# Eighteen dots of the first token tile handed to GpSimd and ScalarE, earlier row fetches, and sixteen mid tokens in a hybrid decoder block

## What is computed

```
h = rmsnorm(x, g_ffn)
q = (h @ w_q) -> 8 heads x 2 halves of 128
v1, i1 = top_k(q0 . k1, 16);  v2, i2 = top_k(q1 . k2, 16)
sc, pos = top_k(v1[:, None] + v2[None, :], 16)     # 16 experts per head, 128 per token
gate = softmax(sc)
x += sum over the 128 experts e of  gate_e * gelu(h . u[e]) * v[e]
```

## Time and profile before

| | us |
|---|---|
| median of 3 runs | 1643.03 (1640.15 to 1643.32) |
| time of the profiled execution | 1643.77 |
| its span, first to last instruction | 1642.0 |
| PE busy | 1600.6 (97%) |
| DVE busy | 1056.9 (64%) |
| ACT busy | 430.1 (26%) |
| POOL busy | 672.0 (41%) |
| moved by DMA | 479.82 MB, mean 292 GB/s |

### The profile page before, as it was taken

One profiled execution on the slowest core, in us unless ns is written; L12 is line 12 of the kernel. 1 busy time (PEld: TensorE's weight loads), 2 busy tenths in 40 slices (PEclk: granted clock), 3 DMA queues, 4 the chain that ended last, 5 costly groups with the idle time before them and its releaser, 6 DMA issues.

```text
span 1642.0 us, 18540 instructions
## 1 busy us (share of the span) xinstructions
PE 1600.6 (97%) x6364; PEld 1053.6 (64%) x6364; DVE 1056.9 (64%) x2437; ACT 430.1 (26%) x1271; POOL 672.0 (41%) x715
## 2 busy tenths in 40 slices
PE   8999999999999989999999999999999999999998
PEld 6446444446786778989989999984444444444443
DVE  2012444431279899998988999996655566667555
ACT  2003444350110211111167877760000000000013
POOL 0002445440001474466745555555434335447530
PEclk9999999999999999999999999999999999999999
DMA  5424111105545899999999999999999999999962
GB/s 173 144 85 146 40 39 39 40 27 166 157 148 167 338 378 375 409 400 387 392 394 409 409 407 409 406 403 392 409 409 409 409 409 410 409 409 398 409 227 103
DMA packets 133274, 479.82 MB, mean 292 GB/s; under 512 B 14859, under 2 KB 15883, under 8 KB 133180
## 3 DMA queue, kind: packets, MB, share of 16 engines
q0 software_dynamic: 74880, 272.66, 42.2%
q1 hardware_dynamic: 58300, 205.97, 33.6%
HBM read 475.38 MB, written 3.19 MB: 291 GB/s over the span
## 4 chain that ended last, share of the span: by engine, by line
PE 72%; DVE 15%; issue 4%; DMA 4%; POOL 3%; ACT 1%; DVEq 0%; SPq 0%; POOLq 0%; ACTq 0%
PE psum L1948 27%; PE psum L1929 9%; DVE arena L1355 7%; PE psum L1739 6%; PE psum L1615 4%; DMA arena<-in_u,eidx 4%; PE psum L1763 3%; PE psum L1815 3%; PE psum L1775 3%; PE psum L1916 3%; PE psum L1858 2%; PE psum L1699 2%; PE psum L1714 2%; POOL arena L609 1%; PE psum L1685 1%
## 5 line engine op out<-in xcount | busy, mean ns | idle before, releaser
L1929 PE MATMUL psum<-arena 128*128 128x248 f32 x2048 | 444.6, 375 | 10.4 <-ACT arena L782 6.8
L1948 PE MATMUL psum<-arena 128*128 128x512 f32 x1024 | 441.8, 594 | 2.7 <-DVE arena L1413 2.7
L1929 PEld LDWEIGHTS psum<-arena 128*128 128x128 f32 x2048 | 386.1, 191 | 50.0 <-issue 12.6
L609 POOL DMA_INDIRECT arena<-in_u,eidx x256 | 256.2, 1001 | 371.9 <-DVE arena L1110 168.0
L609 POOL DMA_INDIRECT arena<-in_v,eidx x256 | 260.7, 1018 | 287.0 <-DVE arena L1390 172.0
L1948 PEld LDWEIGHTS psum<-arena 128*128 128x128 f32 x1024 | 194.9, 191 | 248.3 <-issue 246.0
L1355 DVE CUSTOM_DVE_ANT_0 arena<-psum,arena 128x1024 f32<-128x1024 f32 x256 | 303.5, 1221 | 30.9 <-DMA arena<-in_u,eidx 18.9
L1390 DVE SCALAR_TENSOR_TENSOR arena<-arena,wts 128x1024 f32<-128x1024 f32 x175 | 222.9, 1286 | 109.5 <-DMA arena<-in_v,eidx 101.7
L598 POOL TENSOR_SCALAR arena<-arena 128x256 f32<-128x256 f32 (+4 forms) x128 | 105.9, 846 | 250.9 <-DVE arena L1064 191.7
L1739 PE MATMUL psum<-arena 128*128 128x512 f32 x256 | 118.4, 605 | 0.0
L1815 PE MATMUL psum<-arena 128*128 128x256 f32 x512 | 113.0, 379 | 0.2
(11 more groups left out here) (222 smaller groups left out, 1449.9 us busy)
## 6 DMA issues: line engine op xcount, KB each, us to landing
arena<-in_ut SPq DMA_DIRECT2D x128, 512.0 KB
arena<-in_vd SPq DMA_DIRECT2D x128, 512.0 KB
arena<-in_wpack SPq DMA_DIRECT2D x105, 512.0 KB
arena<-in_u,eidx POOLq DMA_INDIRECT x256
arena<-in_v,eidx POOLq DMA_INDIRECT x256
arena<-in_w_pg SPq DMA_DIRECT2D x8, 512.0 KB
arena<-in_x SPq DMA_DIRECT2D x4, 512.0 KB, 4.9
arena<-bias_rows SPq DMA_DIRECT2D x8, 256.0 KB, 5.5
```

Source lines behind the costliest of these rows:

```text
L609: G.indirect_dma_start(out=row_slot(n), out_offset=None, in_=table, in_offset=bass.IndirectOffsetOnAxis(ap=picks, axis=0)).then_inc(row_ga ...
L1929: last = T.matmul(chunk_scores(c), u[:, k * P:(k + 1) * P], h2T1[:, k, 0:DN], start=(k == 0), stop=(k == KC - 1))
L1948: last = T.matmul(ps[VALUE_BANK[t] + h], mixed[:, c, t * P:(t + 1) * P], stream[:, c % SRING, h * HALF:(h + 1) * HALF], start=(c == 0), st ...
```

## The change

Eighteen dots of tile 0 (`SHARED_DOTS`) are no longer VectorE's. GpSimd multiplies the row with the tokens in place (`row_times`), and ScalarE sums the product by a Copy with an accumulator (`sum_row`). Twelve of them are the first twelve rows; ScalarE sums rows 0 to 6 after `heads_evac(0)`, rows 7 to 9 before `heads_evac(1)`, the others inside it. The slots are taken in a new order, so that the first rows go to slots that are free before the merge is done, and each first fetch waits only for the merges that its slot needs (`gates_gone`). The merges are moved ahead of a part of the top-k work on VectorE. `MID` goes from 8 to 16, so the dense scores have 240 columns and 8 more rows of `u` are gathered, 528 rows in all where there were 520. `EARLY_DOTS` is 144, and the steps of the top-k work lie 5 rows apart from row 12 on. `hn[0]` and `hn[1]` change places, since GpSimd needs `hn[0]` longer. PE's values wait for each late chunk when they come to it, and no longer for all. The dense results are added at k = 111 and 112, and the tail's pieces around them move along. Two `gate_exp` on ScalarE move from chunks 28 and 46 to 31 and 47.

```diff
-EARLY_DOTS = 142
+EARLY_DOTS = 144
+SHARED_DOTS = (0, 1, 2, 3, 4, 5, 6, 7, 8, 9, 10, 11, 18, 23, 28, 33, 38, 43)
+FIRST_DOTS = 12
+SUMMED_AT = ((10, 11), (18,), (23,), (28,), (), (33,), (38,), (43,))
+EARLY_ORDER = (0, 1, 5, 6, 7, 2, 3, 4)
+MIX_ORDER = (0, 1, 5, 2, 3, 4)
-MID = 8
+MID = 16
-DOT_OF_STEP = [2 + 6 * s if s < SPARSE_STEPS else 2 + SPARSE_STEPS + 5 * s for s in range(TOP_UNITS)]
+DOT_OF_STEP = [FIRST_DOTS + 5 * s for s in range(TOP_UNITS)]
...
+        gates_gone = (KC + 2, KC + 4, KC + 6, 2 * KC, 2 * KC, 0, 0, 0)
...
             def fetch(n, table, picks):
                 last_user = row_last_in_slot(n)
-                if last_user is not None:
-                    pool.wait_ge(row_used, last_user + 1)
+                if last_user is None and gates_gone[slot_of(n)]:
+                    pool.wait_ge(merged, gates_gone[slot_of(n)])
+                if last_user in SHARED_DOTS:
+                    pool.wait_ge(row_summed, SHARED_DOTS.index(last_user) + 1)
+                elif last_user is not None:
+                    pool.wait_ge(row_used, vector_rows(last_user) + 1)
...
                 if n == 0:
-                    pool.wait_ge(merged, 2 * KC)
                     pool.wait_ge(experts_known, 1)
...
+            def row_times(n):
+
+                if n == 0:
+                    pool.wait_ge(rows_normed, TILES + 1)
+                pool.wait_ge(row_gathered[slot_of(n)], 16 * times_filled(n))
+                G.tensor_tensor(row_slot(n), row_slot(n), hn[0], ALU.mult).then_inc(row_times_token, 1)
+
             for n in range(2 * NG * COLS + MID):
                 gather(n)
+                if n == 4:
+                    row_times(0)
+                    row_times(1)
+                if 2 <= n - 3 < FIRST_DOTS:
+                    row_times(n - 3)
+                if n - 5 >= FIRST_DOTS and n - 5 in SHARED_DOTS:
+                    row_times(n - 5)
...
+            def sum_row(n):
+                act.wait_ge(row_times_token, SHARED_DOTS.index(n) + 1)
+                col = PICK_ORDER[n]
+                A.activation(row_slot(n), row_slot(n), ACT.Copy, accum_out=dots[:, 0, col:col + 1]).then_inc(row_summed, 1)
...
                     if p:
                         score_evac(h, p - 1)
+                    if h:
+                        for n in SUMMED_AT[p]:
+                            sum_row(n)
...
             heads_evac(0)
+            for n in range(7):
+                sum_row(n)
             peer_norm(2, 4)
...
             turned_evac(h2T1, 1)
+            for n in range(7, 10):
+                sum_row(n)
             heads_evac(1)
...
-            pair_up(0, 4, 8)
             merge(1, UP_FIRST)
             merge(1, UP_FIRST + 1)
+            pair_up(0, 4, 8)
+            merge(1, UP_FIRST + 2)
+            merge(1, UP_FIRST + 3)
             top_pairs(0, 4, 8)
             number_low(0, 1)
             publish(0, 4, 8, 0, 8)
-            merge(1, UP_FIRST + 2)
-            merge(1, UP_FIRST + 3)
...
             for k in range(EARLY_DOTS):
-                dot(*divmod(k, COLS))
+                if k not in SHARED_DOTS:
+                    dot(*divmod(k, COLS))
...
-                if k == 104:
+                if k == 111:
                     add_dense(2)
-                if k == 105:
+                if k == 112:
                     add_dense(3)
...
-            pe.wait_ge(dense_gelu, CHUNKS)
+            pe.wait_ge(dense_gelu, CHUNKS - 1)
             pe.wait_ge(mix_applied, MID_FIRST)
             pe.wait_ge(mix_copied, WG)
-            pe.wait_ge(late_applied, CHUNKS - 1 - FIRST_MIX)

             def values(c, t):
+                if t == 0 and c > FIRST_MIX:
+                    pe.wait_ge(late_applied, c - FIRST_MIX)
                 for h in range(2):
+                    if c == 0 and t == 0 and h == 1:
+                        pe.wait_ge(dense_gelu, CHUNKS)
```

More of the change, by code:

```diff
@@ L187, in build, with vector_rows @@
         low_slots += -(low_slots - EARLY_DOTS) % MIX_SLOTS
-        first_mix_slot = EARLY_DOTS % SLOTS % MIX_SLOTS
+        assert EARLY_DOTS % SLOTS == 0
         def slot_of(n):
             if n < EARLY_DOTS:
-                return n % SLOTS
+                return EARLY_ORDER[n % SLOTS]
             if n < low_slots:
-                return (first_mix_slot + n - EARLY_DOTS) % MIX_SLOTS
-            lap, place_in_lap = divmod(n - low_slots, SLOTS)
-            return place_in_lap if place_in_lap >= MIX_SLOTS else (first_mix_slot + place_in_lap) % MIX_SLOTS
+                return MIX_ORDER[(n - EARLY_DOTS) % MIX_SLOTS]
+            place_in_lap = (n - low_slots) % SLOTS
+            return place_in_lap if place_in_lap >= MIX_SLOTS else MIX_ORDER[place_in_lap]
+        gates_gone = (KC + 2, KC + 4, KC + 6, 2 * KC, 2 * KC, 0, 0, 0)
+        def vector_rows(n):
+            return n - sum(1 for d in SHARED_DOTS if d < n)
         def u_row(i):
@@ L253, in build @@
         hn = [None] * TILES
-        for t in (2, 3, 0):
+        for t in (2, 3, 1):
             hn[t], ra = place(ra, [D])
-        scr = hn[0]
+        scr = hn[1]
         vals, idxu = [None] * 2, [None] * 2
@@ L267, in build @@
         assert ra <= EARLY_HOME and EARLY_HOME + 2 * D <= 120 * DT - 1808
-        hn[1], _ = place(120 * DT, [D])
+        hn[0], _ = place(120 * DT, [D])
         h2T1, h2e = place(H2, [KC, HT])
@@ L398, in build @@
         row_used = sem("row_used")
+        row_times_token = sem("row_times_token")
+        row_summed = sem("row_summed")
         rows_stashed = sem("rows_stashed")
@@ L498, in chain @@
             return 2 * c - 4, 2 * c - 2, 8, NCAND
-        match_rooms = (hn[0], hn[2], hn[3])
+        match_rooms = (hn[1], hn[2], hn[3])
         def matches(t, c):
@@ L669, in _ @@
                     after_low, after_high = [DOT_OF_STEP[step + x] + SLOTS for x in (2, 3)]
-                    if n == (SLOTS - 1 if t == 1 else DOT_OF_STEP[step - 1] + SLOTS):
+                    if n == (FIRST_DOTS + 4 if t == 1 else DOT_OF_STEP[step - 1] + SLOTS):
                         number_pairs(t)
@@ L853, in gelu_dots @@
             def gelu_dots(t):
-                act.wait_ge(row_used, u_row(COLS * (t + 1) - 1) + 1)
+                act.wait_ge(row_used, vector_rows(u_row(COLS * (t + 1) - 1) + 1))
+                act.wait_ge(row_summed, len(SHARED_DOTS))
                 A.activation(dots[:, t, :], dots[:, t, :], ACT.Gelu_apprx_tanh).then_inc(gelu_ready, 1)
@@ L931, in _ @@
                 if c == MID_GELU:
-                    act.wait_ge(row_used, MID_AT + MID)
+                    act.wait_ge(row_used, vector_rows(MID_AT + MID))
                     A.activation(mid_dots, mid_dots, ACT.Gelu_apprx_tanh).then_inc(mid_gelu, 1)
-                if c == 28:
+                if c == 31:
                     gate_exp(2)
-                if c == 46:
+                if c == 47:
                     gate_exp(3)
@@ L1371, in sum_early @@
                 dve.wait_ge(row_gathered[slot_of(n)], 16 * times_filled(n))
-                dve.wait_ge(row_used, n)
+                dve.wait_ge(row_used, vector_rows(n))
                 if k == 0:
@@ L1467, in _ @@
                     gates(1)
-                if k == EARLY_DOTS - 16:
+                if k == 130:
                     gates(2)
@@ L1546, in _ @@
                     tail_out(0)
-                if k == 104:
+                if k == 111:
                     add_dense(2)
-                if k == 105:
+                if k == 112:
                     add_dense(3)
                     tail_scale(1)
-                if k == 107:
+                if k == 114:
                     tail_turned(1)
                     tail_scale(2)
-                if k == 108:
+                if k == 115:
                     tail_turned(2)
-                if k == 120:
+                if k == 124:
                     tail_add(1)
-                if k == 122:
+                if k == 126:
                     tail_out(1)
@@ L1898, in mid_rows @@
             def mid_rows():
-                pe.wait_ge(row_used, COLS)
+                pe.wait_ge(row_used, vector_rows(COLS))
                 for k in range(KC):
```

5 lines of the change are left out of this document (2 added, 3 removed).

## The result

The changed kernel takes 1655.67 us (median of 4, 1654.84 to 1657.66) where the kernel before took 1643.17 beside it (1640.15 to 1645.41): ratio 1.0073, 95% interval 1.0058 to 1.0089. It is 12.5 us slower; 15.1 us less were forecast. Its span is 1655.9 against 1642.0.

What follows compares the result with a forecast made beforehand. PE and the DMA engines were both taken to run at their limit for 1000 us. Gains of 10 + 0.5 + 4.6 + 0 = 15.1 us off a median of 1643.0 gave 1628, range 1623 to 1634.

Steps and rivals of the forecast that it cites:

- Two waits on ScalarE: ScalarE's sums before and inside the second half's copies: dense chunks near 614 and 622, 3 us PE can just spare.
- rival C: In heads_evac(1), ScalarE waits for GpSimd's products; dense chunks start 20 us late, giving 1648; chance 0.11.
- Earlier fetches: Row fetches from 500 instead of 526.98: 6 to 7 rows ahead near 549, 8.3 us of DMA time.
- Less work on VectorE: Before the mixing: eighteen dots, 20.6 us, off VectorE; 4.4 us of unused DMA time won back.
- The port: SBUF interfaces shared by GpSimd and VectorE: no run showed how they hold each other up; nothing booked.
- The moved gate_exp cost nothing: ScalarE's gate exponentials, moved in the program: hidden under the chunks, cost nothing.
- MID = 16: Dense chunks and mixing: 6.9 us less PE on chunks 0 to 61, first mix at 829, 0.5 us booked in mixing.
- Rival A: PE is all that counts, the DMA keeping up by filled slots in the mixing: 21.6 us gained, 1621; chance 0.15.
- Values: Joint from mixing into values, waiting per late chunk: 10.6 us becomes 7.9, 4.6 us booked, bounds 2.7 and 4.6.
- rival B: Bytes are paid at the end, rows 5 us late for the dense adds: 1635 to 1640; chance 0.18.
- Dense adds: At row 111, near the values' end: adds just in time, 0 booked, bounds 0 and a loss of 5 us.

Runs made afterwards that it cites:

- e3: The changed kernel with only rows 18, 23, 28, 33, 38 and 43 shared, VectorE making rows 0 to 11; 1655.68 us, ratio 1.0080.
- e16: The changed kernel with only rows 0 to 11, 18, 23 and 28 shared; 1650.71 us, ratio 1.0041.
- e2: The changed kernel with only rows 0 to 11 shared, the six later dots back on VectorE; 1643.82 us, ratio 1.0005.
- e1: The changed kernel with no shared dots, VectorE making all 144 early dots; 1643.39 us, ratio 1.0009.
- e9: e2 with GpSimd's product reading one operand and a constant instead of two operands, output not the layer's; 1651.19 us, ratio 1.0051.
- e4: The changed kernel with VectorE's gates(0) and gates(1) after row 56 in place of row 40; 1652.46 us, ratio 1.0059.
- e17: The kernel before with 144 early dots for 142, nothing else; 1649.16 us, ratio 1.0028.
- e6: The kernel before with the values' wait per late chunk, and SP's two residual reloads twelve value blocks later; 1641.16 us, ratio 0.9989.
- e10: e2 with SP's two reloads of the residual moved twelve value blocks later; 1646.75 us, ratio 1.0020.
- e13: The kernel before with 48 waits added on counts long met, 16 each on PE, VectorE and ScalarE; 1642.42 us, ratio 0.9999.

## Why the prediction was wrong

*"Two waits on ScalarE" failed, and made the kernel slower.* I gave the relay 3 us, by counting one fetch and product after the other from row 14 at 549, so that the first dense chunk started at 614. A product was near the forecast (2.35 to 2.37 us for 2.17). But VectorE's last merge ended at 525.2 and not at 520, and a pair of fetch and product took 3.5 to 4.7 us, 3.94 in the mean of eight, and not 3.4: row 14 went out at 557.0. So 8 of the 12.1 us by which the first dense chunk missed its forecast were there at row 14 already. Row 43, the last fetch ahead of row 38's product, went out at 620.5. In the kernel before it went out at 618.2; I never set my count beside that, though it was there to be counted. Six waits of 6.3 to 12.2 us came out, and the dense chunks, set at 614 and 622, are at 626.1 and 634.1. This is rival C in its outcome, at a price of 12.5 us in the median (it said 5, by 20 us of lateness less 15 of cover); it had 0.11. Its fetches "that themselves wait for slots" are not what the trace shows: the waits for slots shrank from 21.2 to 3.0 us, and what held the products back was GpSimd's own queue, busy 53.0 of 60 us from 546 to 606 where it had been busy 43.8. e3 shows the relay alone, e16 a good half of it. The forecast also left out that the gates of row 40 stand behind the last sum.

*The gains failed too.* The forecast missed by 27.7 us. 11.9 of them lie between e2 (1643.82), the change without the six later dots, and the change. The other 15.8 are gains that were forecast and that e2 does not have either: its first mix is at 837.0, 1.9 us sooner than before and not 10, and its time is that of before. The next paragraphs are about these.

*"Earlier fetches" failed.* The first fetch is at 502.63 (forecast 500). Twelve rows are out at 546 and row 14 goes out at 557.0, not at 549. Of a lead of 6 to 7 rows there were 4, and GpSimd's products had eaten it by 606. In e2, without the relay, the count at 606 is 39, just that of before. The 8.3 us of lead, the largest term of the sum, did not exist past the next stretch.

*"Less work on VectorE" gained nothing.* VectorE's 20.6 us went, but the idle DMA time was not won back: 310 and 383 GB/s where 342 and 395 stood. Without the six sums (e2) it is 318 and 403. The term of 4.4 us was guessed from an average; GpSimd's queue, which issues every row, was the thing loaded. In e2 VectorE does reach the dot of row 141 5.7 us sooner than before (830.3 for 836.0), but two early rows more and PE's wait for VectorE stand behind it.

*The port.* I wrote that no run shows how the two engines hold each other up, and took 0. VectorE's merges and norm lay on PE's path there, and the turn came 7.4 us late. It cost nothing that the runs show, since PE had 5.93 us of waiting ahead of the dense chunks anyway (e2 starts them at 613.3, and takes as long as e1, which has no product there). The Trainium skill, page "SBUF — State Buffer", section "Who interferes with whom", calls the pair of ports that VectorE and GpSimd share an exclusive lock; by that VectorE waits for the rest of the product (1.64 us) and then takes its own 1.28, together 2.92, and the trace agrees within 0.2 us (2.74). The page counts every GpSimd operation that reads SBUF; the one-operand product, begun first, did not block the same operation here (1.28 us in e9), and the measurement decides.

*"The moved gate_exp cost nothing"* is doubtful. For tiles 0 and 1 the place in the program is the same, and I had not counted them, but it lies behind the sums: VectorE's 8.17 us, and 3.2 us of time in e4, which is not clear of the scatter. VectorE's gates of tiles 2 and 3 moved as well, from row 126 to 130, which I had not named; PE waited 2.73 us for them at 828.52, and no run tests it.

*MID = 16.* The mixing step is 4.31 us at 401 GB/s, as forecast near its byte bound, not the 4.13 of PE. Rival A falls. The 0.5 us was not there (+0.9). The two early rows cost 2.3 to 7.1 in e17, against which the tokens gain 5 to 6.

*Values.* From the last mix to the first value matmul 7.4 us (forecast 7.9), and the first matmuls run without a stall: the term of 2.7 to 4.6 us was right where it was measured, 3.2, and worthless at the end, since the fifth value block stands behind the reloads (1.88 us, then some us at half clock) and one near the end comes late (1.46). The heading of rival B, the bytes are paid at the end, fits this; its time does not.

*Dense adds* were just in time, as forecast: VectorE adds at 1591.34 without a wait, and the tail is 62.4 us for 62.3.

No version beat the kernel before by more than 0.2%; the best, e6, is 0.11% below it with an interval that holds 1.

## What to carry to other kernels

A relay over three engines (fetch, product, sum) costs not its own busy time but everything that stands ahead of it in each engine's queue, paid by whatever stands behind the waiting instruction. Before a wait is put into a queue that PE drains through, count the instructions ahead of the awaited one in the trace of the kernel before, add the new ones, and compare the pace with PE's (here 8.5 to 14.3 us against 7.8). Where the transfers are full for a thousand microseconds, a gain at a joint counts only if fewer bytes are due behind it; count fetches issued by each stage's end, not when the first one goes out.

## What the hardware showed unexpectedly

- GpSimd's product of two 128x1024 float32 operands takes 2.36 us, the same with one operand and a constant 2.77, up to 3.62 beside VectorE (e9).
- A two-operand product held VectorE operations that ran beside it: 2.74 us for 1.28, one small operation 3.03 for 0.17, and a cast of one operand too, 2.39 for 0.18 (533.90). Maxima and a reduction between 509.5 and 514, beside two such products, kept their times (0.87 us for four maxima, 0.86 before). Beside a one-operand product the first of these kept its 1.28.
- With the DMA engines full and GpSimd issuing a row every 1.25 us, ScalarE's next Gelu sometimes comes many microseconds after its input, for no cause that the trace names. In e17:
```profile
827.23 0.38 ACT L866 ACTIVATE arena<-psum 128x248 f32<-128x248 f32 x1 [13.14 <-remote]
...
827.75 6.33 PE L1929 MATMUL psum<-arena 128*128 128x248 f32 x16 [7.52 <-issue]
```
PE then idles 7.5 us, and its clock is at half for some 10 us (822.8 to 833.1). The kernel before has such waits of 5.83 and 6.77 us near 820, e10 of 11.51 and 8.87. The same work in e13 has none and takes as long as the kernel before, so the short ones may cost nothing. What they wait for was not tried and stays open; the long ones may be a part of what e10 and e17 lose.
